# When the norm and rotation of two query groups are placed in the instruction order of a two-block transformer kernel

## The chip, the cores and the metric

The kernel runs on one core of one Trainium2 chip. The metric is the device time of one launch, in microseconds (us). The time of the kernel before is the median of three runs.

The engines are named as in the profile: PE is TensorE (PEld its weight loads), DVE is VectorE, ACT is ScalarE, POOL is GpSimd, SP is SyncE, whose queue issues the DMA transfers. Each runs its own instruction stream in order, and waits on semaphores for the others.

## What is computed

Sequence 256, width 2048, batch 1, all in fp32. The first block is gated linear attention beside a dilated attention, then a gated feed-forward layer. The second is two residual layers: retention with a convolution, and last a sliding-window attention. The change touches that last layer only:

```python
def odd_mixer(h, w_in, q_norm_w, k_norm_w, sinks, w_out, pos):
    proj = h @ w_in                       # (256, 2048) @ (2048, 4608)
    q, k, v, gate = split(proj)           # 32 query heads, 4 key and value heads, of 64
    q = rope(rms_norm_2(q.reshape(b, s, 32, 64), q_norm_w), pos)
    k = rope(rms_norm_2(k.reshape(b, s, 4, 64), k_norm_w), pos)
    o = swa_sinks(q, k, v, sinks)         # softmax over a window of 128, with a sink
    return (o * silu(gate)) @ w_out       # (256, 2048) @ (2048, 2048)
```

## The kernel before

**The matmuls.** Each weight matrix streams through the core once. It is cut into units of 2 x 128 rows by 512 columns (512 KB). For accuracy a unit is split in two parts: ACT makes the high part `wh` (`cut`, L1336), DVE subtracts it from the raw weights and gets the low part `wl` (`cut`, L1589). PE then does 12 matmuls with it (`mul`, L1153 to L1155): high by high, low by high, high by low, for two row tiles of 128 and two halves of the unit. `wh` and `wl` have three buffers, so ACT cuts unit u when PE has ended unit u - 3. There are 661 units. The last layer's are 557 to 628 (input) and 629 to 660 (output). In the output product units 629 to 644 use the first 8 of the 16 row tiles of its left operand, for four column blocks, and units 645 to 660 the last 8, four units per block. So unit 647 is the first to use tiles 12 and 13, unit 648 the first to use 14 and 15.

**The order.** The engines' streams are written from one list, `plan.order`, which class `Plan` makes. `lay` goes through the units; per unit there are two slots, one before each half of its matmuls. In each slot (`step`) generators in lanes may `say` pieces of other work. A `yield n` lets n slots pass. `Plan` keeps an estimate of the time that ACT and DVE are behind (`through`, with costs from the table `WORK`), and `room(engine, us)` yields slot after slot, at most 6, while the engine is more than `us` behind. Every engine does the pieces of the list in its order; PE does its part of a piece at its place between the matmuls.

**The last attention.** The queries come in four groups of 8 heads (0 to 3), each from 8 units. A group's pieces are said in this order (`after`, kinds `oq` and `og`):

- `oq_evac`: ACT copies the product out of PSUM (`TW<-g`), L1333.
- `on_sq`: ACT squares (`TW<-TW`, 128x1024). `on_sum`: DVE sums (`st<-TW`, L1598). `on_root`: twelve small DVE instructions (`st<-st`, 128x16). `on_norm`: two multiplications on DVE (`TW<-TW,st`).
- `on_rope`, twice: six DVE instructions (four `TW<-TW,A`, two `TW<-TW`).
- `oq_turn`, twice: PE transposes (L1087), ACT copies.
- `og`: ACT takes silu of the gate's product. Only when it is said does lane `att` get this group's heads (`od_heads`).

`od_heads` goes over pairs of heads, four slots to a round. `aqk`: PE makes the scores (L1212, L1214); DVE adds the mask into `PB` and reduces for the maximum (L1592, L1598, L1595). `aexp`: ACT takes exponentials (L1462). `apt`: PE transposes (L1222), ACT copies to `PT`. `apv`: PE multiplies with the values into `ob` (L1238 to L1240). `aw`: two small DVE instructions per four heads (`st<-st` 128x8, RECIPROCAL). `afin`: three DVE instructions (`AW`). The four heads' output is then turned by DVE (`turn`), sent through memory by two kinds of DMA and split (`msent`: `mh` by ACT, `ml` by DVE) as two row tiles of the output product. The last four heads go another way: `mix`, where PE transposes (L1087), ACT copies (`mh<-m`) and DVE subtracts (`ml<-m,mh`), tiles 14 and 15.

`aqk`, `apt`, `oq_turn` and `mix` use three PSUM banks `m0` to `m2` in turn: PE's nth use waits until use n - 3 was read, by DVE after `aqk`, by ACT after `apt` and `oq_turn`.

Of the kernel before, what the change touches and what calls it, by code (L numbers as in the profile page):

```python
# [151 lines left out]
class Plan:  # L152
# [45 lines left out]
        if us:  # L198
            self.through[engine] = max(self.through[engine], self.now) + us

    def room(self, engine, us):

        for _ in range(6):
            if self.through[engine] - self.now <= us:
                break
            yield 1
# [255 lines left out]
            self.say("cmix", "M4", 8 + 4 * j + 2 * h, j, h)  # L462

    def od_norm(self, x):
        for p, n in (("on_sq", 1), ("on_sum", 2), ("on_root", 1), ("on_norm", 2)):
            yield n
            self.say(p, x)
        for k in range(2):
            yield 3 if k else 1
            self.say("on_rope", x, k)  # L470

    def dilated(self):
# [1792 lines left out]
```

How the kernel before makes its waits and increments, by code:

```python
    def wait_ge(self, sem, value):  # L599
        if self.seen.get(sem.num, 0) < value:
            self.e.wait_ge(sem, value)
            self.seen[sem.num] = value
# [478 lines left out]
        def tensor(e):  # L1081
# [1 line left out]
            def four(dst, src):
                on.wait_ge(s_small, 32)
                for c in range(4):
                    last = e.transpose(dst(c), src(c), ident)
                return last
            for p in plan.order:
                kind, a = p[0], p[1:]
                if kind == "warm":
                    on.wait_ge(s_warm, 1)
                    for i in range(9):
                        last = e.matmul(MB[2][:, :], wl[:, 2, 0:128], wl[:, 2, 0:512], start=True, stop=True)
                    last.then_inc(s_warmed, 1)
                elif kind == "mul":
                    u, half = a
                    un = units[u]
                    b = un.block
                    hi, lo = acts_of(b.acts)
                    if u == 0:
                        o = [z[:, :] for z in g2(0)]
                        h, l = wh[:, 0, 0:512], wl[:, 0, 0:512]
                        on.wait_ge(s_hi, 1)
                        on.wait_ge(s_split, 1)
                        for k in range(2):
                            e.matmul(o[k], hi[:, 0, 128 * k:128 * k + 128], h, start=True, stop=False)
                        on.wait_ge(s_lo, 1)
                        for k in range(2):
                            e.matmul(o[k], hi[:, 0, 128 * k:128 * k + 128], l, start=False, stop=False)
```

## Time and profile before

| what | value |
| --- | --- |
| runs | 1907.44, 1907.73, 1907.95 us (median 1907.73) |
| profiled execution | 1908.15 us, its span 1906.1 us |
| PE busy | 1897.1 us of the span |
| DVE busy, ACT busy | 1268.3 us, 1001.3 us |
| PE in the chain that ended last | 97% |

The span is the time between the first and the last instruction that the profiler saw. A row of the timeline says start, duration, engine, line, what is written and read, and in brackets how long the engine sat idle before it and who ended that. PE's clock was granted in full over the whole span.

### The profile page before, as it was taken

The numbers are of one execution on the slowest core, as the hardware profiler recorded it, in microseconds if no ns is written. First come the engines' busy times: TensorE is split into PE (matmuls) and PEld (weight loads), VectorE is DVE, ScalarE is ACT, GpSimd is POOL, SyncE is SP. The second block draws the span as 40 slices with busy tenths as digits, with TensorE's granted clock in tenths as the row PEclk, the third lists the DMA queues.
The fourth block names the chain that finished last, engine by engine and source line by source line (L and its number), as shares of the span: only waits on it lengthen the run. The fifth ranks groups of instructions, "written<-read, shape, count | busy, mean of one in ns | idle before, by whom it ended". The sixth has DMA issues, their size and how long they took to land.

```text
span 1906.1 us, 22784 instructions
## 1 busy us (share of the span) xinstructions
PE 1897.1 (100%) x8667; PEld 1560.9 (82%) x8667; DVE 1268.3 (67%) x1923; ACT 1001.3 (53%) x1409; POOL 14.4 (1%) x32
## 2 busy tenths in 40 slices
PE   9999999999999999999999999999999999999999
PEld 7888887888888888888888888888888888787887
DVE  6676566776666556664466776755766677777875
ACT  6777554454444344443444455654555554665653
POOL 0001000000000000000000000000000000000000
PEclk9999999999999999999999999999999999999999
DMA  9667764686666666665666686665676687555555
GB/s 314 196 200 179 205 182 128 201 260 195 194 194 192 195 192 188 198 196 191 196 192 196 217 270 191 197 190 176 196 211 192 195 260 215 164 169 166 152 169 166
DMA packets 211644, 375.33 MB, mean 197 GB/s; under 512 B 14592, under 2 KB 35376, under 8 KB 211536
## 3 DMA queue, kind: packets, MB, share of 16 engines
q1 hardware_dynamic: 210288, 371.12, 64.1%
q0 software_dynamic: 816, 2.11, 0.8%
q8 instruction: 68, 1.11, 0.2%
q10 hardware_dynamic: 432, 0.66, 0.1%
q14 instruction: 40, 0.33, 0.0%
HBM read 361.50 MB, written 12.33 MB: 196 GB/s over the span
## 4 chain that ended last, share of the span: by engine, by line
PE 97%; DVE 1%; DMA 1%; ACT 0%; issue 0%; SPq 0%; DVEq 0%; ACTq 0%
PE g L1153 31%; PE g L1155 31%; PE g L1154 31%; DMA raw<-in_w_in 1%; PE m L1222 1%; PE ob L1240 0%; PE ob L1239 0%; PE m L1087 0%; DVE wl L1589 0%; PE ob L1238 0%; PE m L1214 0%; PE m L1212 0%; PE m L1306 0%; PE ob L1293 0%; DVE st L1598 0%; PE ob L1287 0%
## 5 line engine op out<-in xcount | busy, mean ns | idle before, releaser
L1589 DVE TENSOR_TENSOR wl<-raw,wh 128x1024 fp32r<-128x1024 f32 (+1 forms) x660 | 802.3, 1217 | 562.2 <-ACT wh L1336 559.2
L1336 ACT ACTIVATE wh<-raw 128x1024 fp32r<-128x1024 f32 (+1 forms) x661 | 695.4, 1053 | 750.1 <-PE g L1155 744.1
L1153 PE MATMUL g<-wh,xh 128*128 128x512 f32 x1886 | 741.4, 393 | 2.3 <-DVE xl L1592 2.2
L1155 PE MATMUL g<-wh,xl 128*128 128x512 f32 x1886 | 734.7, 390 | 0.0
L1154 PE MATMUL g<-wl,xh 128*128 128x512 f32 x1886 | 734.0, 389 | 0.0
L1153 PEld LDWEIGHTS g<-wh,xh 128*128 128x128 f32 x1886 | 354.1, 188 | 81.6 <-issue 9.3
L1155 PEld LDWEIGHTS g<-wh,xl 128*128 128x128 f32 x1886 | 354.0, 188 | 74.6
L1154 PEld LDWEIGHTS g<-wl,xh 128*128 128x128 f32 x1886 | 354.2, 188 | 71.7
L1153 PE MATMUL g<-wh,mh 128*128 128x512 f32 x732 | 287.4, 393 | 0.0
L1155 PE MATMUL g<-wh,ml 128*128 128x512 f32 x732 | 285.0, 389 | 0.0
L1154 PE MATMUL g<-wl,mh 128*128 128x512 f32 x732 | 284.9, 389 | 0.0
L1153 PEld LDWEIGHTS g<-wh,mh 128*128 128x128 f32 x732 | 137.4, 188 | 31.7 <-issue 3.9
L1155 PEld LDWEIGHTS g<-wh,ml 128*128 128x128 f32 x732 | 137.4, 188 | 28.9
L1154 PEld LDWEIGHTS g<-wl,mh 128*128 128x128 f32 x732 | 137.5, 188 | 27.7
L1717 DVE STREAM_TRANSPOSE A<-A 32x256 f32<-32x256 f32 x176 | 76.7, 436 | 2.9
L1589 DVE TENSOR_TENSOR x<-g,x 128x512 f32<-128x512 f32 (+1 forms) x73 | 46.3, 676 | 12.1 <-PE g L1155 6.8
L1333 ACT ACTIVATE A<-g,st 128x512 f32<-128x512 f32 x50 | 31.6, 683 | 28.9 <-PE g L1155 28.9
L1336 ACT ACTIVATE A<-TW 32x256 f32<-32x256 f32 x96 | 39.9, 416 | 1.5
L1336 ACT ACTIVATE mh<-A 128x256 fp32r<-128x256 f32 (+1 forms) x56 | 26.9, 506 | 23.6 <-DVE A L1717 16.4
L1336 ACT ACTIVATE PT<-m 128x384 f32<-128x384 f32 x40 | 18.2, 489 | 38.3 <-PE m L1222 38.3
L1592 DVE SCALAR_TENSOR_TENSOR xl<-A,small,xh 128x128 fp32r<-128x128 f32 (+1 forms) x112 | 34.0, 362 | 6.1 <-ACT xh L1336 6.1
L1589 DVE TENSOR_TENSOR ml<-A,mh 128x256 fp32r<-128x256 f32 (+1 forms) x56 | 28.9, 539 | 13.5 <-ACT mh L1336 13.4
(154 smaller groups left out, 818.3 us busy)
## 6 DMA issues: line engine op xcount, KB each, us to landing
raw<-in_ev_w_in SPq DMA_DIRECT2D x128, 512.0 KB, 3.8
raw<-in_w_in SPq DMA_DIRECT2D x92, 512.0 KB, 4.2
raw<-in_w_gate SPq DMA_DIRECT2D x88, 512.0 KB, 4.4
raw<-in_w_up SPq DMA_DIRECT2D x88, 512.0 KB, 4.4
raw<-in_w_down SPq DMA_DIRECT2D x88, 512.0 KB, 4.8
raw<-in_od_w_in SPq DMA_DIRECT2D x72, 512.0 KB, 4.2
raw<-in_w_out SPq DMA_DIRECT2D x32, 512.0 KB, 4.0
raw<-in_ev_w_out SPq DMA_DIRECT2D x32, 512.0 KB, 4.7
```

What stands on the lines that cost most here:

```text
L1153: e.matmul(o, hi[:, kt, c], h, start=first, stop=False)
L1154: e.matmul(o, hi[:, kt, c], l, start=False, stop=False)
L1155: last = e.matmul(o, lo[:, kt, c], h, start=False, stop=end)
L1222: last = e.transpose(o[:, 128 * c:128 * c + 128], L[:, 128 * c:128 * c + 128], ident)
L1333: return e.activation(o, i, func, scale=scale, bias=bias)
L1336: return e.activation(o, i, AF.Copy, scale=scale)
L1589: return e.tensor_tensor(o, a, b, op)
L1592: return e.scalar_tensor_tensor(out=o, in0=a, scalar=s, in1=b, op0=op0, op1=op1)
L1717: last = e.transpose(dst, src)
```

## The change

`room` gets a bound for the number of slots. `od_norm`, which says the pieces of the norm and rotation of the keys (`"k"`) and of the query groups 0 to 3, calls it ahead of each of its six pieces, with 2 slots for groups 1 and 2 (the second and third group) and 0 slots for the others.

```diff
-    def room(self, engine, us):
-
-        for _ in range(6):
+    def room(self, engine, us, most=6):
+
+        for _ in range(most):
             if self.through[engine] - self.now <= us:
                 break
             yield 1
@@ -462,11 +462,14 @@
     def od_norm(self, x):
+        wait = 2 if x in (1, 2) else 0
         for p, n in (("on_sq", 1), ("on_sum", 2), ("on_root", 1), ("on_norm", 2)):
             yield n
+            yield from self.room("act" if p == "on_sq" else "dve", .6, wait)
             self.say(p, x)
         for k in range(2):
             yield 3 if k else 1
+            yield from self.room("dve", .6, wait)
             self.say("on_rope", x, k)
```

No instruction is added or removed. The list is the same up to `on_sq` of group 1. Groups 1 and 2 then say their later pieces some slots later, and with them `og`; from group 2's on this moves `od_heads` too: heads 16 to 23 (group 2) start five slots later against the units than before, heads 24 to 31 (group 3) too, and `mix` at the end stands right ahead of unit 648 where it stood inside unit 645. In the kernel after the change line numbers are 3 higher from `od_norm` on.

The first place is ACT's stream from `oq_evac` of group 3 (`TW<-g,st`) on. Before:

```order
L1333 ACTIVATE TW<-g,st 128x512 x2
L1336 ACTIVATE wh<-raw 128x1024
L1462 ACTIVATE PB,st<-PB,st 128x128
L1462 ACTIVATE PB,st<-PB,st 128x256
L1333 ACTIVATE st<-st,small 128x2
L1462 ACTIVATE PB,st<-PB,st 128x128
L1462 ACTIVATE PB,st<-PB,st 128x256
L1333 ACTIVATE st<-st,small 128x2
L1333 ACTIVATE TW<-TW 128x1024
L1336 ACTIVATE wh<-raw 128x1024
L1336 ACTIVATE PT<-m 128x384 x2
L1336 ACTIVATE wh<-raw 128x1024
```

After:

```order
L1336 ACTIVATE TW<-g,st 128x512 x2
L1339 ACTIVATE wh<-raw 128x1024
L1336 ACTIVATE TW<-TW 128x1024
L1465 ACT_TABLE_LOAD
L1465 ACTIVATE PB,st<-PB,st 128x128
L1465 ACTIVATE PB,st<-PB,st 128x256
L1336 ACTIVATE st<-st,small 128x2
L1465 ACTIVATE PB,st<-PB,st 128x128
L1465 ACTIVATE PB,st<-PB,st 128x256
L1336 ACTIVATE st<-st,small 128x2
L1339 ACTIVATE wh<-raw 128x1024 x2
L1339 ACTIVATE PT<-m 128x384 x2
```

The table load and the exponentials of group 2's first two heads, which stood ahead of `oq_evac` with a cut between them, now stand behind it, its next cut and the squares; the cut of unit 624 comes behind them all.

The second place is DVE's stream ahead of `on_sum` of group 3 (`st<-TW`, its last row here). Before:

```order
L1589 TENSOR_TENSOR wl<-raw,wh 128x1024 x2
L1592 SCALAR_TENSOR_TENSOR PB<-m,small 128x384
L1598 TENSOR_REDUCE st<-PB 128x1 x2
L1595 TENSOR_SCALAR st<-st 128x2
L1592 SCALAR_TENSOR_TENSOR PB<-m,small 128x384
L1598 TENSOR_REDUCE st<-PB 128x1 x2
L1595 TENSOR_SCALAR st<-st 128x2
L1589 TENSOR_TENSOR wl<-raw,wh 128x1024
L1589 TENSOR_TENSOR st<-st 128x8
L1831 RECIPROCAL st<-st 128x8
L1598 TENSOR_REDUCE st<-TW 128x16
```

After:

```order
L1592 TENSOR_TENSOR wl<-raw,wh 128x1024 x2
L1595 SCALAR_TENSOR_TENSOR PB<-m,small 128x384
L1601 TENSOR_REDUCE st<-PB 128x1 x2
L1598 TENSOR_SCALAR st<-st 128x2
L1595 SCALAR_TENSOR_TENSOR PB<-m,small 128x384
L1601 TENSOR_REDUCE st<-PB 128x1 x2
L1598 TENSOR_SCALAR st<-st 128x2
L1601 TENSOR_REDUCE st<-TW 128x16
```

In both the last `wl` ahead of the sum's neighbours is unit 624's. Before, it came behind the scores of heads 20 and 21; after, the scores of heads 18 and 19 come behind it, and heads 20 to 23 are still to come.

The third place is DVE's stream at the end, from `afin` of the last four heads (`AW`) to the cut of unit 648 and on. Before:

```order
L1589 TENSOR_TENSOR AW<-ob,st 128x512
L1589 TENSOR_TENSOR AW<-AW,A 128x256 x2
L1589 TENSOR_TENSOR wl<-raw,wh 128x1024
L1589 TENSOR_TENSOR ml<-A,mh 128x256 x2
L1589 TENSOR_TENSOR x<-g,x 128x512 x2
L1589 TENSOR_TENSOR wl<-raw,wh 128x1024
L1589 TENSOR_TENSOR ml<-m,mh 128x512
L1589 TENSOR_TENSOR wl<-raw,wh 128x1024 x3
L1589 TENSOR_TENSOR x<-g,x 128x512 x2
```

After:

```order
L1592 TENSOR_TENSOR x<-g,x 128x512 x2
L1592 TENSOR_TENSOR wl<-raw,wh 128x1024 x2
L1592 TENSOR_TENSOR AW<-ob,st 128x512
L1592 TENSOR_TENSOR AW<-AW,A 128x256 x2
L1592 TENSOR_TENSOR ml<-A,mh 128x256 x2
L1592 TENSOR_TENSOR wl<-raw,wh 128x1024
L1592 TENSOR_TENSOR ml<-m,mh 128x512
L1592 TENSOR_TENSOR wl<-raw,wh 128x1024
L1592 TENSOR_TENSOR x<-g,x 128x512 x2
```

The two `ml`, tiles 12 and 13 and tiles 14 and 15, moved two cuts down. The last `x<-g,x` of both pieces is the addition behind unit 648; the one `wl` between the second `ml` and it is unit 650's.

## Rows read from the trace of the kernel before

**Rows 1.** The page: busy time of PE and the others, share of the span, instructions

```profile
PE 1897.1 (100%) x8667; PEld 1560.9 (82%) x8667; DVE 1268.3 (67%) x1923; ACT 1001.3 (53%) x1409; POOL 14.4 (1%) x32
```

**Rows 2.** Waits of PE from 1540 us on: total us, times, longest

```profile
PE m L1222 <- DVE PB L1592: 1.1, 1, 1.1
PE m L1087 <- DVE PB L1592: 0.9, 1, 0.9
```

**Rows 3.** Timeline of ACT, 1700 to 1722 us

```profile
1702.88 1.06 ACT L1336 ACTIVATE wh<-raw 128x1024 fp32r<-128x1024 f32 x1 [1.66 <-PE g L1155]
1706.68 1.06 ACT L1336 ACTIVATE wh<-raw 128x1024 fp32r<-128x1024 f32 x1 [2.74 <-PE g L1155]
1707.76 1.28 ACT L1462 ACT_TABLE_LOAD   x1
1709.05 0.40 ACT L1462 ACTIVATE PB<-PB,st 128x128 f32<-128x128 f32 x1
...
1711.19 0.71 ACT L1336 ACTIVATE mh<-A 128x256 fp32r<-128x256 f32 x2
1711.81 1.24 ACT L1333 ACTIVATE TW<-g,st 128x512 f32<-128x512 f32 x2
1712.94 1.05 ACT L1336 ACTIVATE wh<-raw 128x1024 fp32r<-128x1024 f32 x1
1713.89 1.05 ACT L1333 ACTIVATE TW<-TW 128x1024 f32<-128x1024 f32 x1
...
1721.69 1.06 ACT L1336 ACTIVATE wh<-raw 128x1024 fp32r<-128x1024 f32 x1 [1.53 <-PE g L1155]
```

**Rows 4.** Timeline of DVE, 1714 to 1723 us

```profile
1714.03 1.23 DVE L1589 TENSOR_TENSOR wl<-raw,wh 128x1024 fp32r<-128x1024 f32 x1 [1.27 <-ACT wh L1336]
1715.17 0.55 DVE L1592 SCALAR_TENSOR_TENSOR PB<-m,small 128x384 f32<-128x384 f32 x1
...
1717.91 1.22 DVE L1589 TENSOR_TENSOR wl<-raw,wh 128x1024 fp32r<-128x1024 f32 x1
1719.04 1.21 DVE L1598 TENSOR_REDUCE st<-TW 128x16 f32<-128x1024 f32 x1
...
1722.68 1.22 DVE L1589 TENSOR_TENSOR wl<-raw,wh 128x1024 fp32r<-128x1024 f32 x1
```

**Rows 5.** Timeline of PE, 1715 to 1735 us

```profile
1715.87 0.30 PE L1222 MATMUL m<-small,PB 128*128 128x128 f32 x1 [1.06 <-DVE PB L1592]
...
1722.80 0.33 PE L1238 MATMUL ob<-A,PT 128*128 128x64 f32 x2
...
1724.09 0.94 PE L1222 MATMUL m<-small,PB 128*128 128x128 f32 x6
1724.79 0.47 PE L1153 MATMUL g<-wh,xh 128*128 128x512 f32 x1
...
1734.51 0.63 PE L1087 MATMUL m<-small,TW 128*128 128x128 f32 x4 [0.85 <-DVE PB L1592]
```

**Rows 6.** Timeline of DVE, 1726 to 1732 us

```profile
1726.87 1.24 DVE L1589 TENSOR_TENSOR TW<-TW,st 128x512 f32<-128x512 f32 x2
1728.03 1.22 DVE L1589 TENSOR_TENSOR wl<-raw,wh 128x1024 fp32r<-128x1024 f32 x1
...
1731.31 1.22 DVE L1589 TENSOR_TENSOR wl<-raw,wh 128x1024 fp32r<-128x1024 f32 x1
```

**Rows 7.** Timeline of DVE, 1854 to 1862 us

```profile
1854.60 0.69 DVE L1589 TENSOR_TENSOR AW<-ob,st 128x512 f32<-128x512 f32 x1 [0.28 <-PE ob L1240]
1855.32 0.76 DVE L1589 TENSOR_TENSOR AW<-AW,A 128x256 f32<-128x256 f32 x2
...
1858.32 0.75 DVE L1589 TENSOR_TENSOR ml<-A,mh 128x256 fp32r<-128x256 f32 x2
...
1861.32 0.68 DVE L1589 TENSOR_TENSOR ml<-m,mh 128x512 fp32r<-128x512 f32 x1
```

**Rows 8.** The chain that ended last, 1859 to 1862 us: start, us, what

```profile
1860.07 0.44 PE m L1087 x4
```

## The prediction

> **What bounds the kernel now.** I read the busy times first: PE is busy for 1897.1 us of a span of 1906.1 [rows 1]. No instruction is added or removed, so PE's work stays, and the change can act in one way only: through the time that PE sits idle. Next come PE's waits in the stretch that the change touches. From 1540 us on there are two, 1.06 and 0.85 us, both for DVE's reading of `PB` out of a bank of `m` [rows 2, 5]. So the most that any order of the last layer can win is 1.9 us of 1908, 0.10%. What it can lose has no such bound. The question is then whether PE meets new waits, and for this I follow ACT and DVE, which must cut each unit and empty the banks in time.
>
> **The pace.** ACT's cut is released when PE has ended the unit three before. In a stretch with matmuls alone such releases stand 1.06 + 1.66 = 2.72 us apart, and 1.06 + 2.74 = 3.80 where PE did the scores of two heads in between [rows 3]: a unit costs PE 2.72 us, a pair of `aqk` 1.08. A pair of `apv` takes 1.29 and a pair of `apt` 0.70 [rows 5], a turn 0.44 [rows 8].
> DVE, start to start: `wl` 1.14, then PE may go on with the freed bank 1715.87 - 1715.17 = 0.70 after `PB` starts; a head's scores (1717.91 - 1715.17)/2 = 1.37; `on_sum` and `on_root` together 1722.68 - 1719.04 = 3.64 [rows 4, 5]. `on_norm` 1728.03 - 1726.87 = 1.16, `on_rope` 1731.31 - 1728.03 - 1.14 = 2.14 [rows 6]. `aw`, two small instructions, I estimate at 0.4, since `on_root`'s twelve take the 2.4 us that `on_sum`'s 1.21 leaves of 3.64.
> ACT: `oq_evac` 1.13, a cut 0.95 when another follows, the squares the same; table load and two exponentials 1711.19 - 1707.76 = 3.43; from the start of a cut to the start of its `wl` 1714.03 - 1712.94 = 1.09 [rows 3, 4].
>
> **How the wait of 1.06 came about.** It is the pattern for what follows. Heads 8 and 9 needed the exponential's table; load, exponentials, a split and `oq_evac` stood ahead of a cut on ACT, which so began at 1712.94. DVE had sat idle 1.27 us for it at 1714.03, and only behind this `wl`, in its order, came the `PB` that held the bank [rows 3, 4].
>
> **The change, part by part.**
>
> *Group 1 (heads 0 to 7 run beside it).* Its pieces only go down past work of others, and DVE's prefix ahead of each `wl` and `PB` gets shorter, up to the cut of unit 598. The pieces end up among units 595 to 602, where less is said beside them, and heads 8 on keep their place. No wait before, none after: 0.
>
> *Group 2, the wait of 1.06.* ACT's order is the same up to the cut in question (unit 607; `on_sq` stands behind it). It stays: 0.
>
> *Group 2, the wait of 0.85.* It was a turn of group 2's queries that needed a bank behind `on_rope`, two scores and `wl` on DVE [rows 5, 6]. The turn leaves the place, and `on_rope` and `on_root` no longer stand ahead of those scores as they did. It goes: -0.85.
>
> *Group 3, wait A.* Heads 16 to 23 start five slots later, but `oq_evac` of group 3 hangs on PE's units and does not move. So the table load and heads 16 and 17 fall behind it (the first order rows). I count from the moment T at which PE has ended unit 620. ACT: `oq_evac` 1.13, cut 623 0.95, squares 0.95, 0.13 until that has drained, load and exponentials 3.43, then cut 624, whose `wl` starts 1.09 later: T + 7.68. DVE idles for it, and `PB` of head 18, behind it in the order, starts 1.14 later; PE gets the bank at T + 9.52. PE needs it for the second `apt` of heads 16 and 17: in the wait of 1.06 PE began to wait at 1715.87 - 1.06 = 1714.81, 5.41 after the end of unit 604 (1706.68 + 2.72); here one whole unit more lies between, T + 8.13. Wait A: +1.4.
>
> *Wait B.* Behind `wl` of unit 624 DVE has two scores, then `on_sum` and `on_root`: `wl` of unit 625 starts at T + 7.68 + 3.88 + 3.64 = T + 15.20, and is there 1.22 + 0.15 later (0.15 as from `PB`'s end to PE's start), T + 16.57. After wait A PE has the same pieces as after 1715.87, until it ended unit 607 at 1721.69 [rows 3]: 9.52 + 5.82 = T + 15.3, and it issues the next unit a little before that end, so about 15.2. Wait B: +1.4. Before, unit 625 came only after two more heads' `apv` and `apt`.
>
> *Waits C.* DVE goes on without a gap: from 15.20 `wl` 1.14, norm 1.16, `wl` 1.14, two scores 2.74, rotation 2.14, `aw` 0.4, `wl` 1.14, rotation 2.14, `wl` 1.14, then `PB` of heads 22 (+0.70) and 23 (+1.37): PE has the last bank at T + 30.4. PE from 16.57: unit 625 2.72, `apv` 1.29, `apt` 0.70, unit 626 2.72, `aqk` 1.08, turn 0.44, half of unit 627 1.36, `apv` 1.29, first `apt` 0.35: 28.5. Waits C: +1.9. Then the additions' stretch begins, and DVE catches up.
>
> *Heads 24 to 31.* Scores of heads 26 and 27, an addition and `wl` of unit 639 now follow one another on DVE behind a split that waits for ACT. The same sum gives PE 0.1 and 0.5 us of waiting: +0.6, taken between 0 (it was covered before) and 1.1 (a wait like the one seen).
>
> *The end.* `afin` of the last heads now comes behind the cut of unit 648, which is released when PE ends unit 645, R. `wl` from R + 1.09, `afin` from 2.23, 0.69 + 0.76 long, `ml` of tiles 12 and 13 0.75 [rows 7]: R + 4.4. PE had its last `apv` (1.29) and unit 646 and wants unit 647 at R + 3.8: +0.6. The transposes of `mix` stood 2.5 units, 6.8 us of matmuls, ahead of their user; now unit 648 is next, and nothing covers what follows them. Transposes at 1860.07, `ml` done at 1861.32 + 0.68 = 1862.00 [rows 7, 8]: 1.93 us, of which 0.44 is PE's own work, and 0.1 to get going: +1.6.
>
> **Sum.** -0.85 + 1.4 + 1.4 + 1.9 + 0.6 + 0.6 + 1.6 = +6.65 us on the profiled 1908.15. That execution is 0.42 over the median of 1907.73; the difference belongs on the median: **1914.4 us**.
>
> A rule that bears on wait A. The row shows a table load of 1.28 us with the first exponential 0.01 us behind it (1707.76 + 1.28 = 1709.04) [rows 3]. The Trainium skill (ScalarE: Activation LUTs, What ACT_TABLE_LOAD costs) has about 1283 ns for the load and some 1380 ns of draining besides, at each switch of set. The load agrees, the drain does not show here: ACT's load began 0.02 us after the cut's end. By the page wait A and what follows would be up to 1.4 us larger; by the row it is not, and the row decides.
>
> **The rivals.**
> *Not slower: only the end costs, and DVE has room in group 3.* Point of decision: whether `wl` of unit 624 starts 7.7 us after PE's end of unit 620, or at about T + 3.8, as it would if the load and the exponentials found a gap. Then A, B and C fall away: -0.85 + 0.6 + 2.2 = +2.0, 1909.7 us; if the end too were covered, 1907. For it: DVE is only 67% busy over the span [rows 1]. Against: the order rows put them in ACT's way, and an engine keeps its order. 12%.
> *Faster.* Both waits of before go and none comes: 1907.73 - 1.9 = 1905.8. The order at unit 607 speaks against the first half. 2%.
> *The late work runs on.* Each new wait makes later pieces meet PE at another point; a split that comes back from memory too late for unit 647, or group 1's pieces at unit 598, would add waits of the size seen, three of 1.1: +3.3, 1917.7 us. 14%, half of it beyond the range.
> *The forecast*, all of A to C and the end, in sizes that differ by up to 2.5 us together: 1911.8 to 1917. 72%.
>
> **How the numbers follow.** A measurement of this kernel can tell 0.2%, 3.8 us, from no change. All of the forecast and of the last rival lie beyond 1911.5, 86%; of the small case (1907 to 1911) and the faster one all lies within. I give slower 0.84, same 0.15, faster 0.01. The range must leave out at most 2 in 10: from 1910.5 to 1918.0.
>
> **What the profile after would show.** PE's list of waits from 1540 us on sums to some 8.5 us instead of 1.9. The wait at 1715.9 is still there and the same; the one at 1734.5 is not. A wait of PE `m` (L1225) of 1.4 us for `PB` near 1775, one of `g` (L1156) for `wl` near 1782, one or two for `PB` near 1795; two of `g` for `ml`, 0.6 and 1.6 us, near 1870. DVE idle for `wh` ahead of wait A, and then busy for 24 us on end. Wrong would be: no wait of `g` for `wl` at all (DVE's backlog misjudged), or a long run of waits in group 1.

## The result and the profile after

The kernel after takes 1914.82 us (median of 6 runs, 1914.17 to 1915.91), the kernel before 1907.80 (6 runs, 1907.44 to 1907.95): ratio 1.0038, 95% interval 1.0028 to 1.0048. It is slower by 7.0 us, where 6.65 were forecast.

The profiled execution took 1914.36 us, its span 1912.3. First its page: busy time of the engines, share of the span, instructions; it answers [rows 1].

```profile
PE 1898.7 (99%) x8667; PEld 1562.2 (82%) x8667; DVE 1268.7 (66%) x1923; ACT 1000.7 (52%) x1409; POOL 14.3 (1%) x32
```

The work is the same, and the span is 6.2 us longer: 1.6 of it counts as PE's busy time, 4.6 as its idle time. Next, PE's waits from 1540 us on (total us, times, longest), which answer [rows 2].

```profile
PE m L1225 <- DVE PB L1595: 3.8, 4, 1.4
PE g L1156 <- DVE ml L1592: 2.3, 2, 1.5
PE g L1156 <- DVE wl L1592: 1.6, 2, 1.2
```

Two waits became eight. Their rows in PE's timeline, in order of time:

```profile
1715.38 0.52 PE L1225 MATMUL m<-small,PB 128*128 128x128 f32 x3 [1.06 <-DVE PB L1595]
...
1776.47 0.52 PE L1225 MATMUL m<-small,PB 128*128 128x128 f32 x3 [1.35 <-DVE PB L1595]
...
1783.43 0.50 PE L1156 MATMUL g<-wh,xh 128*128 128x512 f32 x1 [1.23 <-DVE wl L1592]
...
1795.87 0.52 PE L1225 MATMUL m<-small,PB 128*128 128x128 f32 x3 [0.53 <-DVE PB L1595]
1797.24 0.52 PE L1225 MATMUL m<-small,PB 128*128 128x128 f32 x3 [0.85 <-DVE PB L1595]
...
1837.12 0.50 PE L1156 MATMUL g<-wh,mh 128*128 128x512 f32 x1 [0.40 <-DVE wl L1592]
...
1868.39 0.47 PE L1156 MATMUL g<-wh,mh 128*128 128x512 f32 x1 [0.80 <-DVE ml L1592]
...
1873.31 0.47 PE L1156 MATMUL g<-wh,mh 128*128 128x512 f32 x1 [1.50 <-DVE ml L1592]
```

The wait of 1.06 is the one of [rows 5]; the turn's 0.85 is gone. The other seven sum to 6.66 us and stand where the forecast had them: A at 1776, B at 1783, C at 1796 and 1797, unit 639 at 1837, units 647 and 648 at 1868 and 1873.

Now the cause of A. ACT's timeline from the moment T = 1766.94, at which PE had ended unit 620 and `oq_evac` of group 3 could start:

```profile
1766.94 1.27 ACT L1336 ACTIVATE TW<-g,st 128x512 f32<-128x512 f32 x2 [2.48 <-PE g L1158]
1768.09 1.06 ACT L1339 ACTIVATE wh<-raw 128x1024 fp32r<-128x1024 f32 x1
1769.04 1.06 ACT L1336 ACTIVATE TW<-TW 128x1024 f32<-128x1024 f32 x1
1770.12 1.28 ACT L1465 ACT_TABLE_LOAD   x1
1771.41 0.40 ACT L1465 ACTIVATE PB<-PB,st 128x128 f32<-128x128 f32 x1
...
1773.56 1.99 ACT L1339 ACTIVATE wh<-raw 128x1024 fp32r<-128x1024 f32 x2
```

From T on ACT works without a gap, and the cut of unit 624, the first of the two in the last row, starts only at T + 6.62. DVE's timeline shows what this does to it:

```profile
1774.63 1.23 DVE L1592 TENSOR_TENSOR wl<-raw,wh 128x1024 fp32r<-128x1024 f32 x1 [4.22 <-ACT wh L1339]
1775.78 0.55 DVE L1595 SCALAR_TENSOR_TENSOR PB<-m,small 128x384 f32<-128x384 f32 x1
...
1778.51 1.21 DVE L1601 TENSOR_REDUCE st<-TW 128x16 f32<-128x1024 f32 x1
...
1782.15 1.22 DVE L1592 TENSOR_TENSOR wl<-raw,wh 128x1024 fp32r<-128x1024 f32 x1
...
1795.17 0.55 DVE L1595 SCALAR_TENSOR_TENSOR PB<-m,small 128x384 f32<-128x384 f32 x1
...
1796.54 0.55 DVE L1595 SCALAR_TENSOR_TENSOR PB<-m,small 128x384 f32<-128x384 f32 x1
```

It idles 4.22 us for `wh`, starts `wl` of unit 624 at T + 7.69 (forecast T + 7.68) and `wl` of unit 625 at T + 15.21 (forecast T + 15.20), and no row from there to 1797.91 has a bracket (the rows left out included): over 23 us without a gap. So an engine that is 66% busy over the span held PE up four times in 21 us, because it had been made to stand idle just before.

The end of the kernel, from the chain that ended last (start, us, what):

```profile
1859.60 1.24 DVE wl L1592
...
1860.85 0.39 SPq L1082
...
1861.34 5.29 DMA A<-blocks
...
1866.65 0.73 ACT mh L1339 x2
...
1867.48 0.77 DVE ml L1592 x2
...
1868.39 0.47 PE g L1156
...
1871.37 0.45 PE m L1090 x4
...
1871.84 0.61 ACT mh L1339
...
1872.47 0.70 DVE ml L1592
...
1873.31 0.47 PE g L1156
```

In [rows 8] the four transposes of `mix` are a step of 0.44 us in a chain of PE's own work. Here `mix` has 1.94 us from 1871.37 to 1873.31, and nothing of PE's fits in between. And ahead of unit 647 stands a link that the forecast's sum did not have: a `wl` that frees a raw buffer, a weight load on SP's queue that needs it, and behind that the fetch of the attention's output from memory, 5.29 us to its landing.

### The profile page after: what moved, and what is told of

It reads as the page before. It is cut to its first block, busy times and chain, and to the rows that moved or that the text cites. A ratio compares the mean times of both kernels' runs of the same rounds, so it can differ in the third digit from the quotient of the medians.

```text
span 1912.3 us, 22783 instructions
## 1 busy us (share of the span) xinstructions
PE 1898.7 (99%) x8667; PEld 1562.2 (82%) x8667; DVE 1268.7 (66%) x1923; ACT 1000.7 (52%) x1409; POOL 14.3 (1%) x32
## 4 chain that ended last, share of the span: by engine, by line
PE 95%; DVE 2%; ACT 1%; DMA 1%; issue 0%; SPq 0%; DVEq 0%; ACTq 0%
PE g L1156 30%; PE g L1158 30%; PE g L1157 30%; DVE wl L1592 1%; PE m L1225 1%; DMA raw<-in_w_in 0%; PE ob L1242 0%; PE ob L1243 0%; ACT wh L1339 0%; PE m L1090 0%; PE ob L1241 0%; DVE TW L1592 0%; DVE st L1601 0%; PE m L1309 0%; DMA A<-blocks 0%; ACT PB L1465 0%
## 5 line engine op out<-in xcount | busy, mean ns | idle before, releaser
L1158 PE MATMUL g<-wh,xl 128*128 128x512 f32 x1886 | 735.1, 390 | 0.0
L1158 PEld LDWEIGHTS g<-wh,xl 128*128 128x128 f32 x1886 | 354.1, 188 | 74.3
L1158 PE MATMUL g<-wh,ml 128*128 128x512 f32 x732 | 285.2, 390 | 0.0
L1158 PEld LDWEIGHTS g<-wh,ml 128*128 128x128 f32 x732 | 137.5, 188 | 28.9
```

Of the source, the lines that this page charges most:

```text
L1158: last = e.matmul(o, lo[:, kt, c], h, start=False, stop=end)
```

## The experiments

There were eleven runs in three groups, each beside the kernel before on its chip: 1907.59 us in the first (20 runs), 1907.36 in the second (22), 1907.61 in the third (27).

### Which group's delay costs, and whether it is the pieces or the heads

The theory: it is not the norm's later place that costs, but that `og` of group 2 starts heads 16 to 31 five slots later. Four kernels: the delay for the second group alone (g1_only), for the third alone (g2_only), and the kernel before with nothing but later heads, from group 2 on (heads2_late) or from group 3 on (heads3_late).

```diff
 g1_only, against the kernel after
-        wait = 2 if x in (1, 2) else 0
+        wait = 2 if x == 1 else 0
 g2_only, against the kernel after
-        wait = 2 if x in (1, 2) else 0
+        wait = 2 if x == 2 else 0
 heads2_late, against the kernel before, ahead of od_heads' loop (heads3_late: j == 3)
+        if j == 2:
+            yield 5
         for it in range(7):
```

> Only group 1's norm and rotation are said when there is room; group 2's stay as before. Theory (the loss comes from heads 16 to 31 starting five slots later): nothing moves behind unit 602, so PE keeps its two waits of 1.06 and 0.85 us and gets no new one; 1907.8 us, within 0.5 us of before. Rival (late norm pieces of any group push DVE past the cuts near unit 598 and leave a backlog): 1908.5 to 1910, with a wait of PE for wl or PB between 1680 and 1710 us.

> Only group 2's pieces are said when there is room. Theory: the whole loss is here, with the same seven new waits of PE as after the change (6.7 us together) and the wait of 0.85 us gone; 1914.5 us. Rival (group 1 has a part in it): 1911 to 1913.

> The kernel before, its norms all at their old places, but heads 16 to 23 start five slots later (and with them heads 24 to 31 and mix). Theory: the start of the heads is the cause, not the place of the norm pieces, so the waits of the change all come (A 1.4, B 1.2, C 1.4, 0.4, and 0.8 and 1.5 at the end), and the old wait of 0.85 us stays: 1907.8 + 6.65 + 0.85 = 1915.3 us. Rival (group 2's norm pieces, pushed among units 612 to 616, make the backlog): 1909 to 1911, only the waits at the end appear.

> The kernel before, but only heads 24 to 31 start five slots later. Theory: group 3's stretch is as before, so A, B and C do not come; of the new waits only 0.4 us near unit 639 and 0.8 and 1.5 us at units 647 and 648 do, and both old ones stay: +2.7, 1910.5 us. Rival (the end costs nothing by itself and its waits are what is left of group 3's backlog): 1907.8 us and no wait for ml.

Measured: g1_only 1907.75 us (10 runs), ratio 1.0001 [0.9991, 1.0010]; g2_only 1914.53 (5 runs), 1.0037 [1.0023, 1.0050]; heads2_late 1916.14 (4 runs), 1.0044 [1.0029, 1.0059]; heads3_late 1910.48 (10 runs), 1.0016 [1.0007, 1.0025].

PE's timeline of g1_only has the two waits of before and no other:

```profile
1714.98 0.52 PE L1225 MATMUL m<-small,PB 128*128 128x128 f32 x3 [1.07 <-DVE PB L1595]
...
1733.62 0.63 PE L1090 MATMUL m<-small,TW 128*128 128x128 f32 x4 [0.85 <-DVE PB L1595]
```

PE's timeline of heads2_late, where the norm and rotation of every group stand at their old places:

```profile
1734.71 0.63 PE L1089 MATMUL m<-small,TW 128*128 128x128 f32 x4 [0.85 <-DVE PB L1594]
...
1778.43 0.52 PE L1224 MATMUL m<-small,PB 128*128 128x128 f32 x3 [1.35 <-DVE PB L1594]
...
1785.39 0.50 PE L1155 MATMUL g<-wh,xh 128*128 128x512 f32 x1 [1.27 <-DVE wl L1591]
```

The old 0.85 is back, and A, B and C are there in full (1.35, 1.27, 0.53 and 0.85) with no norm moved. So the whole loss comes from the later start of the heads of group 2 and after. The delay of the second group costs nothing; what the change wins, the 0.85, comes from the third group's own later pieces (g2_only has no such wait). heads2_late took 0.8 us more than expected; the section on the sum of the waits comes back to this.

heads3_late took away A to C and kept the end, as expected. One point missed: 0.4 us was expected at unit 639, and there is no wait. In the kernel after, DVE has this ahead of that unit's `wl`:

```profile
1831.23 0.76 DVE L1592 TENSOR_TENSOR ml<-A,mh 128x256 fp32r<-128x256 f32 x2 [3.01 <-ACT mh L1339]
1831.91 0.55 DVE L1595 SCALAR_TENSOR_TENSOR PB<-m,small 128x384 f32<-128x384 f32 x1
...
1833.28 0.55 DVE L1595 SCALAR_TENSOR_TENSOR PB<-m,small 128x384 f32<-128x384 f32 x1
...
1834.65 1.28 DVE L1592 TENSOR_TENSOR x<-g,x 128x512 f32<-128x512 f32 x2
1835.85 2.35 DVE L1592 TENSOR_TENSOR wl<-raw,wh 128x1024 fp32r<-128x1024 f32 x2
```

The split `ml` waits 3.01 us for ACT, and two scores, an addition and the `wl` queue up behind it. This `ml` belongs to a group whose heads are late only where group 2's are. In heads3_late this split began at 1816.79, and the scores' `PB` of heads 26 and 27, from 1825.88 on, had none ahead of them.

### One cause of A to C at a time

after_cut moves the exponentials of heads 16 and 17 (and the table load with them) behind the cut of unit 624. after_sum moves `on_sum` and `on_root` of group 3 behind the cut of unit 625. Both are the kernel after with one call, right behind `self.lay()`.

```diff
+        self.shift([("aexp", "o", 16), ("aexp", "o", 17)], ("cut", 624), True)   # after_cut
+        self.shift([("on_sum", 3), ("on_root", 3)], ("cut", 625), True)          # after_sum
+
+    def shift(self, what, mark, behind=False):
+        for p in what:
+            self.order.remove(p)
+        at = self.order.index(mark) + behind
+        self.order[at:at] = what
```

> The changed kernel, with the exponentials of heads 16 and 17 behind the cut of unit 624 on ACT instead of ahead of it. Theory (wait A is DVE idling for that cut, which stands behind table load and exponentials): DVE's wl of unit 624 starts some 3.4 us earlier, wait A (1.35) is gone, B (1.23) too, since DVE is ahead by 3.4, and C (1.38) shrinks or goes: 1911 to 1912.2 us. Rival (DVE has too much work in this stretch whatever ACT does): A goes, but the same total comes back as B and C; 1914 to 1915.

> The changed kernel, with on_sum and on_root of group 3 behind the cut of unit 625 on DVE instead of ahead of it. Theory: wait B is 3.64 us of sum and root standing ahead of a wl that is due; with the wl ahead B (1.23) goes. C (1.38) grows by what B no longer gives DVE in time, since DVE's total up to head 23's scores is the same: A 1.35, B 0, C 2.6; 1914 to 1915 us. Rival (B is a loss by itself and C is independent of it): 1913.5.

after_cut took 1910.53 us (10 runs), 1.0016 [1.0007, 1.0025]. ACT's timeline of it, and under it DVE's:

```profile
1769.97 1.06 ACT L1346 ACTIVATE wh<-raw 128x1024 fp32r<-128x1024 f32 x1
1771.04 1.28 ACT L1472 ACT_TABLE_LOAD   x1
```

```profile
1771.06 1.23 DVE L1599 TENSOR_TENSOR wl<-raw,wh 128x1024 fp32r<-128x1024 f32 x1 [0.67 <-ACT wh L1346]
```

DVE's idle time for `wh` fell from 4.22 to 0.67 us, and its `wl` starts 3.6 us sooner. A and B are gone and C shrank from 1.38 to 1.01: the loss is 3.2 us (1910.53 - 1907.36, the kernel before beside it) where it was 7.0. So one order of two pieces on ACT was 3.8 of the 7.0 us.

after_sum took 1915.33 us (4 runs), 1.0041 [1.0027, 1.0055]. PE's timeline of it:

```profile
1776.83 0.52 PE L1232 MATMUL m<-small,PB 128*128 128x128 f32 x3 [1.35 <-DVE PB L1602]
...
1786.81 0.52 PE L1232 MATMUL m<-small,PB 128*128 128x128 f32 x3 [1.26 <-DVE PB L1602]
...
1791.13 0.66 PE L1097 MATMUL m<-small,TW 128*128 128x128 f32 x4 [0.18 <-DVE TW L1599]
```

PE no longer waits at unit 625; it waits as long for the next `PB`, which now has the sum and the root ahead of it. The time is 0.3 over the range expected. Moving work within a backlog moved the wait and saved nothing, as both the total of the expectation and the forecast's reading of B (DVE's backlog, not the place of one piece) had it.

### The end

after_tail is the kernel after with the split of tiles 12 and 13 ahead of the last `afin`, and `mix` ahead of unit 647's second half.

```diff
+        self.shift([("msent", "M5", 12, "o", 6)], ("afin", "o", 7))
+        self.shift([("mix", "M5", 14, "o", 7)], ("mul", 647, 1))
```

> The changed kernel, with the split of tiles 12 and 13 ahead of afin of the last heads, and mix ahead of the second half of unit 647 instead of behind it. Theory: the split no longer waits for afin's 1.45 us on DVE, so the wait of 0.80 goes, and half a unit, 1.36 us, covers mix's 1.50: 0.1 to 0.2 left. 1914.8 - 2.1 = 1912.7 us, the waits A to C unchanged. Rival (the split is late because its data come late from memory): the wait of 0.80 stays, 1913.5.

It took 1913.24 us (5 runs), 1.0030 [1.0017, 1.0042]. The wait at unit 648 is gone from the list: half a unit of matmuls now stands between the transposes (1870.14) and the split's first user, which starts at 1872.25, 0.51 us behind the matmul before it where 0.23 is usual. So some 0.3 is left, as expected or a little more. The wait at unit 647 fell to 0.27 only, and `afin` can't be its cause; the time is 0.5 over the expectation. The chain that ended last, of after_tail:

```profile
1862.17 4.76 DMA A<-blocks
...
1866.94 0.73 ACT mh L1347 x2
```

Here the split waits for the fetch to land. This holds across the runs. Where `ml` has `afin` ahead of it and its operand in time, the wait is 0.55 (g2_only, heads2_late, after_cut, after_sum), with fetches of 4.1 to 4.4 us. Where the fetch takes longer than that order hides, it decides: after 5.29 and a wait of 0.80, heads3_late 5.45 and 0.96; with the split moved ahead of `afin`, after_tail 4.76 and 0.27, after_four (below) 6.11 and 1.61. Within each pair the wait grows by what the fetch takes more (0.16 and 0.16; 1.35 and 1.34).

### Keeping the gain without the loss

two_moves is the kernel before with the cut of unit 607 ahead of the split that stood in its way, and group 2's first turn behind unit 610. wait_one gives group 2 one slot ahead of each piece where the change gave two, and group 1 none. one_and_cut has both, wait_one's delay and the move of cut 607. after_four is the kernel after with four moves against A to C, the end and the 1.06.

```diff
 two_moves, on the kernel before
+        self.shift([("cut", 607)], ("msent", "M5", 2, "o", 1))
+        self.shift([("oq_turn", 2, 0)], ("mul", 610, 1), True)
 wait_one, against the kernel after
-        wait = 2 if x in (1, 2) else 0
+        wait = 1 if x == 2 else 0
 one_and_cut, on wait_one
+        self.shift([("cut", 607)], ("msent", "M5", 2, "o", 1))
 after_four, on the kernel after
+        self.shift([("cut", 607)], ("msent", "M5", 2, "o", 1))
+        self.shift([("aexp", "o", 16), ("aexp", "o", 17)], ("cut", 624), True)
+        self.shift([("msent", "M5", 12, "o", 6)], ("afin", "o", 7))
+        self.shift([("mix", "M5", 14, "o", 7)], ("mul", 647, 1))
```

> The kernel before with two single moves in the list: the cut of unit 607 ahead of the split msent of tiles 2 and 3 and of group 2's oq_evac, and the first turn of group 2 one slot later, behind the second half of unit 610's matmuls. Theory (each of the two old waits is one engine being one piece late): both go, no new one comes, 1907.8 - 1.9 = 1905.9 us. Rival (the backlog is only pushed on): the waits show up again at the next bank or cut, 1907.5 to 1908.

> Only group 2, and at most one slot later ahead of each piece instead of two. Its second turn then stands at unit 614 and og at unit 615, and heads 16 to 23, 24 to 31 and mix keep the places of the kernel before. Theory (the loss is the heads' late start, the gain the turn's distance from the two scores): the wait of 0.85 us goes, that of 1.06 stays, no new one: 1907.5 - 0.9 = 1906.6 us. Rival (later norm pieces cost DVE something wherever they land): 1907.5 or more, with a new wait for wl or PB between 1735 and 1760 us.

> One slot for group 2 alone, as in the run with that label, and the cut of unit 607 ahead of the split and oq_evac. Theory: no wait of PE from 1540 us on, 1907.5 - 1.9 = 1905.6 us, the same as the two single moves. Rival: 1906.5, if the earlier cut only helps in the order of before.

> The changed kernel with four moves: the cut of unit 607 ahead of a split and oq_evac of group 2, the exponentials of heads 16 and 17 behind the cut of unit 624, the split of tiles 12 and 13 ahead of afin, and mix half a unit earlier. Theory (each wait is a local matter of order): left are the waits that these moves do not touch, 0.16 and 0.85 at unit 627, 0.37 at unit 639 and up to 0.3 at unit 648, 1.7 us in all, as against 1.9 before the change: 1907.4 us. Rival (waits removed early come back later): 1908.5 or more.

Measured: two_moves 1905.56 us (11 runs), 0.9990 [0.9982, 0.9999]; wait_one 1906.23 (11 runs), 0.9993 [0.9984, 1.0002]; one_and_cut 1904.84 (11 runs), 0.9987 [0.9978, 0.9996]; after_four 1908.05 (10 runs), 1.0003 [0.9994, 1.0012].

In wait_one the slots of the six pieces add up: the first turn of group 2 moves from unit 610 to 613 and `og` from unit 612 to 615. Heads 16 to 31 keep their places, since lane `att` is still at heads 8 to 15 then, and PE's list has one wait from 1540 us on:

```profile
1715.55 0.52 PE L1225 MATMUL m<-small,PB 128*128 128x128 f32 x3 [1.06 <-DVE PB L1595]
```

In two_moves and one_and_cut it has none there. one_and_cut is the fastest version found, 2.8 us under the kernel before; with two_moves it is one of the two whose intervals lie below 1. So one slot ahead of each piece of group 2 is useful, and the second brings the loss: it moves `og` to unit 618, past the place where heads 16 and 17 started (unit 617), and with it everything that hangs on it.

after_four missed its expectation at one place. PE's timeline of it, and under it ACT's:

```profile
1865.06 0.47 PE L1166 MATMUL g<-wh,mh 128*128 128x512 f32 x1 [1.61 <-DVE ml L1602]
```

```profile
1863.33 0.72 ACT L1349 ACTIVATE mh<-A 128x256 fp32r<-128x256 f32 x2 [2.51 <-DMA A<-blocks]
```

At most 0.3 was expected behind this, at unit 648, and nothing here; ACT stood idle 2.51 us for a fetch of 6.11. The orders of ACT and DVE were mended there, that of the DMA queue was not. The profiled execution is also the slowest of its runs (1909.66, the median 1908.05); that the fetch's length makes the spread of this kernel is likely, but not shown.

### Do the waits add up to the time?

The table sets the sum of PE's waits from 1540 us on against the sum of before, 1.91 in two waits. The third column adds 0.15 us for each wait more or less (why, stands in the next section). The fourth takes one stretch out of each trace, from the start of ACT's cut of unit 595 to that of its last cut, and sets it against the 228.69 us of before (1894.63 - 1665.94); in no kernel does PE wait between 30 us and this stretch. The last column takes medians, against the kernel before beside them.

| kernel | waits, sum | with 0.15 each | stretch of the trace | medians |
| --- | --- | --- | --- | --- |
| after | 8, 7.72 | +6.7 | +6.7 | +7.0 |
| g2_only | 8, 7.48 | +6.5 | +6.5 | +6.9 |
| heads2_late | 9, 8.34 | +7.5 | +7.8 | +8.6 |
| heads3_late | 4, 4.38 | +2.8 | +2.9 | +2.9 |
| after_cut | 6, 4.49 | +3.2 | +2.9 | +3.2 |
| after_sum | 9, 7.68 | +6.8 | +6.6 | +8.0 |
| after_tail | 7, 5.68 | +4.5 | +6.3 | +5.9 |
| after_four | 3, 2.83 | +1.1 | +1.5 | +0.4 |
| wait_one | 1, 1.06 | -1.0 | -1.3 | -1.4 |
| two_moves | 0 | -2.2 | -1.9 | -1.8 |
| one_and_cut | 0 | -2.2 | -2.3 | -2.8 |

But for after_tail the waits give the stretch to within 0.5 us. The two causes add up in it: the late heads alone +7.80 (heads2_late), the late pieces alone -1.26 (wait_one, with one slot instead of two), together +6.54, and g2_only, which has both, +6.53. Between stretch and medians lie the spread of the executions and that of the kernel before, whose profiled one is 0.4 to 0.8 us over the medians of its groups; a part of it are PE's waits in the first 25 us, long before anything that these kernels differ in (3.6 us in the trace of before, 2.4 in that of after). So of the 1.1 and 1.2 us by which the medians of heads2_late and after_sum exceed the third column, 0.3 and nothing are in their stretches.

after_tail's 1.8 us are another matter, and no wait. PE's clock fell there. First the two matmuls at 1798 us in its timeline, then the row of the stretch 1797 to 1799 us (busy us and instructions of PE, PEld, DVE, ACT, POOL, then PE's granted clock, the DMA engines' share and GB/s):

```profile
1798.11 0.63 PE L1166 MATMUL g<-wh,xl 128*128 128x512 f32 x1
1798.54 0.63 PE L1164 MATMUL g<-wh,xh 128*128 128x512 f32 x1
```

```profile
1797.00:1799.00 2.00, 2.00 (x8) 1.61 (x7) 1.96 (x4) 1.50 (x7) 0.00 (x0) 0.50 0.34 119
```

Right behind the two waits of C the granted clock is 0.50, the lower of its two levels (1.2 and 2.4 GHz), for some 3 us, and matmuls start 0.43 us apart instead of 0.23. Against the kernel after, the cuts of after_tail are 0.04 us late at unit 628 and 1.49 from unit 632 on. The trace of the kernel after shows the full clock there, but three of its six runs have a mean granted clock of 0.999 and took 1915.23 to 1915.91 us, the three at 1.000 took 1914.17 to 1914.41. No run of the kernel before in the three groups is below 1.000, and of the others only g2_only (1 of 5), after_sum (1 of 4) and after_tail (2 of 5) have such runs; all of them have the waits A to C or as many in their place (heads2_late has them too, and none of its 4 runs is below 1.000). That it is the same fall each time is likely, but only after_tail's trace shows it.

## Why the prediction was right

**The mechanism.** Each wait that the forecast named is there, with the releaser that it named, and none besides. g2_only, heads2_late and heads3_late show that the late heads cause them, after_cut that ACT's order at the table load starts A and B, after_sum that B is a backlog. The rival in which only the end costs (1909.7) needed `wl` of unit 624 at about T + 3.8; it started at T + 7.69. after_cut made very nearly that case: `wl` at T + 4.15 and 1910.5 us, A and B gone, but a C of 1.01 left.

**The terms.** Group 1 nothing: g1_only differs from before by 0.2 us of 1907.6. The wait of 1.06 stays, the one of 0.85 goes: both so. A 1.35 (forecast 1.4), B 1.23 (1.4), C 1.38 (1.9), unit 639 0.40 (0.6), unit 647 0.80 (0.6), unit 648 1.50 (1.6). So the new waits sum to 6.66, not 7.5, and with the 0.85 gone the list grew by 5.81, not 6.65. Still the time came out at the forecast.

**What made up for it.** From PE's resumption after the wait of 1.06 to the release of the last unit's cut the kernel before took 1894.63 - 1715.87 = 178.76 us, the kernel after 1900.88 - 1715.38 = 185.50: 6.74 more, 0.93 over the waits' 5.81. The bracket counts idle time from the end of the matmul before. But matmuls overlap: in the chain of after one unit's matmuls follow each other every 0.23 us, and each lasts 0.39 by the costliest groups of its page (L1158: 735.1 us for 1886, 390 ns). A wait so costs its bracket and the lost overlap, 0.39 - 0.23 = 0.16; six waits more make 0.9. By this count C, which the forecast worked out from start to start, is not 1.38 either: PE had the last bank at T + 30.30 (forecast 30.4) and, resumed at T + 16.49, had 11.9 us of work up to it, which leaves 1.9. The forecast's list of "some 8.5 us" of waits mixed the two ways of counting, and its sum of time did not. The 0.15 is a mean: two_moves lost two waits of 1.91 us and won 1.88, wait_one lost one of 0.85 and won 1.26, and why is open.

The clock has a part in the medians: the three runs at the full clock have a median of 1914.36 us, 6.6 over before, and the other three, with the lower mean clock, lift it to 1914.82. The forecast had no term for the clock; by the runs at the full clock it is as near as by all.

**The bound on what can be won.** "The most that any order of the last layer can win is 1.9 us" is too low: one_and_cut won 2.3 us in the stretch and 2.8 by the medians. The brackets leave out the lost overlap, 0.3 for two waits; the rest is open.

**The mis-sized term.** At unit 647 the forecast charged `afin` of the last heads ahead of the split: +0.6. That order alone gives 0.55 (four kernels). It met this with two slips that cancel: 1.29 and 2.72 us put PE at R + 4.0, not R + 3.8 (g2_only: R = 1864.00, the wait begins at R + 3.98), and the 0.15 from `ml`'s end to PE's start is left out (it resumes at R + 4.53, forecast 4.4). The 0.80 is the fetch's, which the forecast had only in the rival "a split that comes back from memory too late for unit 647"; that element of the rival is true, at 0.25 us of the 1.1 that it was given. Its other elements (group 1's pieces, other matmuls met) didn't come.

**The sizes taken between ends.** Unit 639 was taken at 0.6 between 0 and 1.1, and measured 0.40; the end's 1.6 at unit 648 came from the steps of [rows 7, 8] and measured 1.50.

**The table load.** ACT's load begins 0.02 us after the end of the squares (1769.04 + 1.06 = 1770.10) and takes 1.28, and the first exponential starts 0.01 us behind it, as in [rows 3]. The Trainium skill (ScalarE: Activation LUTs, What ACT_TABLE_LOAD costs) adds some 1380 ns of draining to each switch. This case's trace doesn't agree: the sum without it met `wl` of unit 624 to 0.01 us.

## What to carry to other kernels

A piece may be said later for nothing, but ask what is started by its end: here `og` let 16 heads in, and five slots of theirs cost 7.8 us where the late pieces won 1.3. Where the bounding engine has 1.9 us to win, look at the in-order neighbours of every wait before moving anything, and move the one piece in the way: two moved pieces took away both waits of before. Add a wait from start to start, with the overlap that it breaks, and put the queue that fetches data into the order too: mending ACT's and DVE's order left a fetch as what PE waits for. And look at the granted clock of the stretch before calling a rest unexplained: short waits close together can cost more than their length.

## What the runs showed of the hardware

**The fetch from memory.** It is long and uneven against its size. The last fetch of 256 KB took from issue to landing 4.76, 5.29, 5.45 and 6.11 us in four kernels and 4.1 to 4.4 in four others; the median of the 39 such fetches in the kernel after is 5.0:

```profile
A<-blocks SPq DMA_DIRECT2D x39, 256.0 KB, 5.0
```

The Trainium skill (DMA: Bandwidth & Descriptors, Anatomy of one DMA — SWDGE (gpsimd) path) gives 2.0 us plus the bytes at 436 GB/s, which makes an estimate of 2.6 us for this size. No row of this size comes near it (3.8 to 6.3 us in the kernel after). Three rows of 128 KB do: 2.1, 2.1 and 2.2 us, where the same sum makes an estimate of 2.3; a unit of the last weights, 512 KB, lands in 4.4 us, sooner than this fetch of half its size. The fetch shares the DMA engines with the weight stream (195 GB/s over the span), and it goes by another path than the page's, so neither which of the two makes the difference nor why the same fetch varies by 2 us is settled.

**PE's clock behind waits.** In after_tail PE's idle times of 0.55 and 0.85 us, 0.5 us of work apart, were followed by some 3 us at half the clock, which cost 1.5 us; in the kernel after the same two waits (0.53 and 0.85) were followed by none in the profiled execution. What decides between the two is not shown.
